# A fused two-block transformer kernel: the first attention's scores as two stacked products of high and low parts

## The chip, the cores and the metric

The kernel runs on one core of one Trainium2 chip. The metric is the device time of one execution in microseconds (us), median of the runs, lower is better. TensorE is called PE below, its weight loads PEld, VectorE DVE, ScalarE ACT, GpSimd POOL and SyncE SP, as in the profile.

## The reference, cut to what matters

Two transformer blocks run one after the other on x of 1024 positions by 1024 channels, all in float32. The part that is changed is the attention of the first block: 8 heads of 64 channels, three dilated windows mixed by their softmax denominators.

```python
z = h @ w_in
q, k, v, zu, zv = jnp.split(z, [D_ATTN, 2 * D_ATTN, 3 * D_ATTN, 3 * D_ATTN + D_SGU], axis=-1)
q = q.reshape(B, S, N_ATTN_HEADS, HEAD_DIM) * (HEAD_DIM ** -0.5)
...
DILATED_BRANCHES = ((128, 1), (512, 4), (2048, 16))
s = jnp.einsum('brnqhd,brnkhd->brnhqk', qb, kw).astype(jnp.float32)
s = s + bias.transpose(2, 0, 1)
...
p = jnp.exp(s - m)
...
w = jax.nn.softmax(jnp.stack(lses, axis=0), axis=0)
return jnp.einsum('ibsh,ibshd->bshd', w.astype(q.dtype), jnp.stack(outs, axis=0))
...
mix = jnp.concatenate([attn, sgu], axis=-1) @ w_out
x = x + rms_norm(mix, g_post_mix)
```

The projection behind that attention (`@ w_out`) is the weight stream that the kernel calls OUT1.

## The kernel before, in words

Everything stands in one program with its waits written by hand; each engine goes through its own list in order. Large products are split: a weight slab `raw` is turned by ACT into a high part `whi` (L768) and by DVE into a low part `wlo` (L1715), both of the reduced-precision type fp32r, and PE adds three fp32r products per tile (L1219, and L1237 where two slabs are interleaved). Slabs alternate between two buffers of each.

The first attention runs over 8 heads with 8 steps each, n = 8h + d. Its pieces, by step:

- **Scores** (L1413): per step two plain float32 products of 128x256, keys `KA` as the weights, queries `QA` as the moving data. For d below 4 (called near here) the 128 keys of a weight load lie side by side; for d of 4 and more (far) they lie 4 elements apart (`far_keys`). Both tiles hold the head's 64 channels in partitions 0 to 63, a row of ones and the guard's row in partition 64 and zeros above.
- **Bias and exponent**: DVE subtracts the bias strip from the scores (L1899), ACT takes the exponent (L913) into one of four `PT` buffers.
- **Weighted values** (L1433 near, L1438 far): three steps behind the scores, float32, summed over a head's steps in TP.
- **Guard** (L1386 on PE, L1885 on DVE): twelve steps ahead, PE forms rounded scores of one 128-row tile and DVE takes a bound from them. After 8 tiles PE (L1393) and ACT (L881, the tile `ROW`) make a row of bounds, and POOL copies it into `QA` by four DMAs (L628). All guard tiles after the first ten share one PSUM tile, so a guard product waits until DVE took the one before. Guards end 12 steps before the last score.

At each head's start ACT has extra work that stands in its list between the exponents: at d = 1 `operands(h+1)` copies keys and queries of the next head (L872, L873), at n = 10, 26 `round_pair` (L861, L862), at d = 2 `sums_copy(h-1)` takes the sums of the head before out of TP (L890), at d = 3 `inverse(h-1)` (L896, L899). PE may not start the weighted values of d = 0 before the first half of that `sums_copy` is done. POOL scales a finished head (L606), moves values (L614) and loads bias and strips.

Around the attention: ACT makes the high part of OUT1's first slab before it, of the second at n = 40; DVE makes their low parts before it and at n = 58.

Of the kernel before, what the change touches and what calls it, by code (L numbers as in the profile page):

```python
# [142 lines left out]
def build(nc, slabs, ada, xT, vecs, lnrow, sgu_wT, rel_bias, positions, consts, hot, outT, dbg=None):  # L143
# [60 lines left out]
    KA = [at(f"KA{b}", [P, S], A_XT + 4096 * b) for b in range(2)]  # L204
    QA = [at(f"QA{b}", [P, S], A_XH + 8192 + 4096 * b) for b in range(2)]
# [120 lines left out]
    zeros_set = sem("zeros_set")  # L326
# [234 lines left out]
    def _(pool):  # L561
# [29 lines left out]
        pool.wait_ge(turned, 16)  # L591
        for b in range(2):
            pool.memset(KA[b][DH:P, :], 0.0).then_inc(zeros_set, 1)
            pool.memset(QA[b][DH:P, :], 0.0).then_inc(zeros_set, 1)
        pool.wait_ge(zeros_set, 4)
        for b in range(2):
            pool.memset(KA[b][DH:DH + 1, :], 1.0).then_inc(ones_set, 1)

# [18 lines left out]
        pool.wait_ge(ones_set, 2)  # L617
# [5 lines left out]
        for h in range(HEADS):  # L623
            pool.wait_ge(row_made, h + 1)
            if h >= 2:
                pool.wait_ge(st_ready, NT * (h - 1))
            for c in range(4):
                pool.dma_start(QA[h % 2][DH:DH + 1, c * 2 * P:(c + 1) * 2 * P],  # L628
                               ROW8[h % 2][0:NT, c * 32:(c + 1) * 32]).then_inc(row_loaded[h % 2], 16)
# [127 lines left out]
    def _(act):  # L757
# [88 lines left out]
        for j in range(4):  # L846

            g = IN1 + S_V1 + j
            hi_next(g, g % 2, g // 2)
# [15 lines left out]
        def operands(h):  # L865
# [26 lines left out]
        def inverse(h):  # L892
# [5 lines left out]
            aseq.wait(act)  # L898
            act.activation(ATTN[h // 2][own, :], OL[h % 2][other, :], ACT.Exp, scale=-1.0).then_inc(inverse_ready, 1)  # L899

        def dilated_attention():

            act.preload_act_table_set("natural_log_exp_and_others")
            operands(0)
# [3 lines left out]
            for n in range(NT * HEADS):  # L908
# [7 lines left out]
                if n == 40:  # L916
                    hi_next(OUT1, OUT1 % 2, OUT1 // 2)
# [6 lines left out]
                if n in (52, 60):  # L924
                    attended(n // 8 - 6)
            sums_copy(HEADS - 1)
# [15 lines left out]
        round_pair(0)  # L942
        turned_hi(4, 4, 16)
# [260 lines left out]
    def _(pe):  # L1204
# [18 lines left out]
        def product_pair(g, xh, xl, fresh, base, order=range(KT_N)):  # L1223

            pe.wait_ge(lo_ready, g + 2)
            for one in (g, g + 1):
                pe.wait_ge(psum_free[one % 2], one // 2 + 1)
            for step in range(KT_N + PAIR_LAG):
                if step < KT_N:
                    pe.wait_ge(fresh, base + step + 1)  # L1230
                for one, at_k in ((g, step), (g + 1, step - PAIR_LAG)):
                    if not 0 <= at_k < KT_N:
                        continue
                    b, k = one % 2, order[at_k]
# [1178 lines left out]
```

## Time and profile before

| | |
|---|---|
| median of 3 runs | 2792.73 us (2788.41 to 2807.02) |
| profiled execution, its own time | 2793.15 us |
| its span | 2791.4 us |
| busy: PE, DVE, ACT, POOL | 2641.2, 1351.2, 836.0, 251.5 us |
| attention, first score to last | 320 to 501 us of the span |

Busy shares are averages; which engine is waited for is read in the stretch itself. A matmul's duration includes its latency, so products that follow each other overlap, and the distance between starts is what one costs. A plain float32 product is two records in the trace, an fp32r one is one record; both carry their own weight load. The profile prints f32 for either.

### The profile page before, as it was taken

To read this page: it belongs to the slowest core of one execution; us is meant where nothing else is said; L and a number is where in the kernel's file an instruction comes from. 1 tells how busy PE (TensorE), PEld (TensorE's weight loads), DVE (VectorE), ACT (ScalarE), POOL (GpSimd) and SP (SyncE) were. 2 spreads that over 40 slices of the span, in tenths; PEclk is the share of its full clock that TensorE was granted. 3 is DMA by queue.
4 is the path that set the end of the run, shared out by engine and by line. 5 is a ranking of instruction groups with operands and counts; after the bars stand their busy time and mean duration, and the time that the engine had idled before them with its cause. 6 is when DMAs were issued, how large, how long until landed. Compare 5 with 4: busy or idle time off the path is not lost.

```text
span 2791.4 us, 28672 instructions
## 1 busy us (share of the span) xinstructions
PE 2641.2 (95%) x11363; PEld 2088.6 (75%) x11363; DVE 1351.2 (48%) x1585; ACT 836.0 (30%) x1083; POOL 251.5 (9%) x269
## 2 busy tenths in 40 slices
PE   5999999989999999999999988898999999999996
PEld 3887667867888888888765766665878888888884
DVE  5242666356334343345748878786453232232333
ACT  3211345333112021121325575435332021120221
POOL 0000222002111121121001000211000000000000
PEclk9999999999999999999899998999999999999997
DMA  3211110214222222231310111001111111111111
GB/s 111 89 46 50 42 55 32 68 60 151 91 80 87 76 90 83 76 105 61 136 41 5 46 39 39 4 8 50 67 38 53 46 46 53 45 53 45 46 53 68
DMA packets 50376, 169.68 MB, mean 61 GB/s; under 512 B 7544, under 2 KB 11128, under 8 KB 50232
## 3 DMA queue, kind: packets, MB, share of 16 engines
q1 hardware_dynamic: 32544, 104.27, 11.4%
q0 software_dynamic: 17728, 63.98, 6.7%
q8 instruction: 72, 1.18, 0.2%
q14 instruction: 32, 0.25, 0.0%
HBM read 152.05 MB, written 12.68 MB: 59 GB/s over the span
## 4 chain that ended last, share of the span: by engine, by line
PE 81%; DVE 9%; ACT 5%; issue 4%; DMA 0%; SPq 0%; DVEq 0%; POOL 0%; ACTq 0%; POOLq 0%
PE G L1219 61%; PE G L1237 4%; PE G L1413 2%; PE TP L1642 2%; ACT TK L1071 2%; PE G L1560 1%; PE TP L1433 1%; PE TP L1386 1%; PE TP L1257 1%; DVE JUNK L2245 1%; PE G L1576 1%; ACT T L1057 1%; PE TP L1280 1%; PE TP L1438 1%; DVE wlo L1715 1%
## 5 line engine op out<-in xcount | busy, mean ns | idle before, releaser
L1219 PE MATMUL G<-XH,whi 128*128 128x512 f32 x1712 | 539.2, 396 | 15.2 <-DVE wlo L1715 13.1
L1219 PE MATMUL G<-XL,whi 128*128 128x512 f32 x1712 | 529.9, 391 | 0.0
L1219 PE MATMUL G<-XH,wlo 128*128 128x512 f32 x1712 | 529.8, 391 | 0.0
L768 ACT ACTIVATE whi<-raw 128x1024 fp32r<-128x1024 f32 x184 | 193.8, 1053 | 732.6 <-PE G L1219 671.0
L1219 PEld LDWEIGHTS G<-XH,whi 128*128 128x128 f32 x1712 | 319.8, 189 | 86.5 <-DVE wlo L1715 15.2
L1219 PEld LDWEIGHTS G<-XL,whi 128*128 128x128 f32 x1712 | 322.7, 189 | 67.8
L1219 PEld LDWEIGHTS G<-XH,wlo 128*128 128x128 f32 x1712 | 322.7, 188 | 67.8
L1219 PE MATMUL G<-UH,whi 128*128 128x512 f32 x1024 | 316.9, 391 | 0.0
L1219 PE MATMUL G<-UL,whi 128*128 128x512 f32 x1024 | 315.6, 389 | 0.0
L1219 PE MATMUL G<-UH,wlo 128*128 128x512 f32 x1024 | 315.5, 389 | 0.0
L1715 DVE TENSOR_TENSOR wlo<-raw,whi 128x1024 fp32r<-128x1024 f32 x184 | 224.3, 1220 | 149.4 <-ACT whi L768 149.1
L1219 PEld LDWEIGHTS G<-UH,wlo 128*128 128x128 f32 x1024 | 192.3, 188 | 40.0
L1219 PEld LDWEIGHTS G<-UL,whi 128*128 128x128 f32 x1024 | 192.3, 188 | 40.0
L1219 PEld LDWEIGHTS G<-UH,whi 128*128 128x128 f32 x1024 | 191.1, 188 | 38.6
L2026 DVE SCALAR_TENSOR_TENSOR XT<-G,mod,XT 128x1024 f32<-128x1024 f32 x32 | 41.1, 1285 | 249.1 <-PE G L1219 249.1
L2012 DVE TENSOR_TENSOR USQ<-RELU 128x1024 f32<-128x1024 f32 x32 | 39.2, 1225 | 192.2 <-ACT RELU L999 192.1
L995 ACT ACTIVATE RELU<-RELU 128x1024 f32<-128x1024 f32 x32 | 34.0, 1062 | 243.1 <-DVE RELU L2006 224.0
L1071 ACT ACTIVATE TK<-SC,cand 128x512 f32<-128x512 f32 (+2 forms) x93 | 82.8, 892 | 67.2 <-DVE cand L2132 67.2
L2026 DVE SCALAR_TENSOR_TENSOR XT<-G,XT 128x1024 f32<-128x1024 f32 x24 | 29.4, 1225 | 151.3 <-PE G L1219 151.3
L1991 DVE TENSOR_REDUCE RED<-ADA 128x128 f32<-128x1024 f32 x48 | 95.0, 1979 | 0.0
L999 ACT ACTIVATE RELU<-G 128x1024 f32<-128x1024 f32 x32 | 32.9, 1028 | 205.0 <-PE G L1219 205.0
L1885 DVE CUSTOM_DVE_ANT_0 JUNK<-TP,BIAS 128x1024 bf16<-128x1024 f32 x54 | 66.2, 1226 | 50.5 <-PE TP L1386 50.5
(304 smaller groups left out, 3195.2 us busy)
## 6 DMA issues: line engine op xcount, KB each, us to landing
raw<-slabs SPq DMA_DIRECT2D x184, 512.0 KB, 3.4
ADA<-ada POOLq DMA_DIRECT2D x48, 512.0 KB, 3.8
x_spill<-XT POOLq DMA_DIRECT2D x2, 4096.0 KB, 12.9
BIAS<-tab_spill POOLq DMA_DIRECT2D x8, 960.0 KB, 4.9
XT<-xT SPq DMA_DIRECT2D x8, 512.0 KB, 10.0
XRE<-xT POOLq DMA_DIRECT2D x8, 512.0 KB, 3.9
XRE<-x_spill POOLq DMA_DIRECT2D x8, 512.0 KB, 3.7
XT<-x_spill POOLq DMA_DIRECT2D x1, 4096.0 KB, 13.8
```

Source lines behind the costliest of these rows:

```text
L768: act.activation(whi[b][:, :, :].rearrange("p k n -> p (k n)"), raw[b][:, :], ACT.Copy).then_inc(hi_ready, 1)
L995: act.activation(RELU[:, :], RELU[:, :], ACT.Square).then_inc(usq_ready, 1)
L1071: t_counted.inc(act.activation((TK1, TK2)[t_counted.n % 2][:, 0:w], SC[:, score_at(TOPK_TILE + n):score_at(TOPK_TILE + n + 1)], ACT.Sign, ...
L1219: last = pe.matmul(G[b][:, half, :], w[b][:, k, :], x[:, k, half * HALF:(half + 1) * HALF], start=(at_k == 0 and n == 0), stop=(at_k == KT ...
L1237: last = pe.matmul(G[b][:, half, :], w[b][:, k, :], x[:, k, half * HALF:(half + 1) * HALF], start=(at_k == 0 and n == 0), stop=(at_k == KT ...
L1413: last = pe.matmul(G[n % 4 // 2][:, n % 2, j * 2 * P:(j + 1) * 2 * P], keys, queries, start=True, stop=True)
L1642: pe.matmul(TP[1][:, u % 2, :], VO2[r][:, c, :], PT2[n % 4][:, :], start=(c == 0), stop=(c == i)).then_inc(p2_used, 1)
L1715: dve.tensor_tensor(wlo[b][:, :, :].rearrange("p k n -> p (k n)"), raw[b][:, :], whi[b][:, :, :].bitcast(F32).rearrange("p k n -> p (k n)" ...
L1885: dve.tensor_tensor_reduce(out=JUNK1[:, :], in0=flat(guard_out(p)), in1=BIAS[h % 2][:, 896 - i * P:896 - i * P + S], scale=1.0, scalar=HIG ...
L1991: dve.tensor_reduce(RED[a % 2][:, :], ADA[a % 2][:, :, :].rearrange("p k n -> p n k"), AX.X, ALU.add).then_inc(ada_red, 1)
L2012: dve.tensor_tensor(USQ[:, :], RELU[:, :], RELU[:, :], ALU.mult).then_inc(usq_ready, 1)
L2026: ins = dve.scalar_tensor_tensor(out=XT[:, m - 8, :], in0=Gf[b], scalar=scale(m - 8), in1=XT[:, m - 8, :], op0=ALU.mult, op1=ALU.add)
```

## The change

Scores are no longer a plain float32 product. Keys and queries are split into an fp32r high part and a low part, and two fp32r products of 128 partitions are added: `KH` (high keys, the same in both halves of the partitions) with `QHL` (high queries in the head's own half, low queries in the other), and `KLO` (low keys in the own half, the row of ones in the other) with `QHR` (high queries in the own half, the guard's row in the other). `KLO` and `QHR` lie where `wlo` and `whi` are, so OUT1's slabs are split at the attention's end.

```diff
-            pool.memset(KA[b][DH:P, :], 0.0).then_inc(zeros_set, 1)
-            pool.memset(QA[b][DH:P, :], 0.0).then_inc(zeros_set, 1)
+            other = halves(b)[1]
+            one = ones[other, :].unsqueeze(1).broadcast_to([DH, NT, P])
+            for t in (KLO, QHR):
+                pool.tensor_tensor(t[b][other, :].rearrange("p (t c) -> p t c", c=P), one, one, ALU.subtract).then_inc(zeros_set, 1)
...
+        def low_parts(h):
+
+            own, other = halves(h)
+            pool.wait_ge(ones_set, 4 if h else 2)
+            if h:
+                pool.wait_ge(values_ready, max(h, 2))
+            if h > 2:
+                pool.wait_ge(att_scaled, h - 2)
+            pool.wait_ge(operands_ready, 4 * (h + 1))
+            pool.tensor_tensor(KLO[h % 2][own, ::-1], KT[own, h // 2, :], KH[h % 2][own, ::-1].bitcast(F32),
+                               ALU.subtract).then_inc(lows_ready, 1)
+            in_class = lambda t: t.rearrange("p (c u) -> p c u", c=4)
+            pool.wait_ge(lows_ready, 2 * h + 1)
+            pool.tensor_tensor(in_class(QHL[h % 2][other, :]), by_class(QT[own, h // 2, :]),
+                               in_class(QHL[h % 2][own, :].bitcast(F32)), ALU.subtract).then_inc(lows_ready, 1)
...
         for h in range(HEADS):
+            if h:
+                low_parts(h)
             pool.wait_ge(row_made, h + 1)
...
-                act.wait_ge(operands_ready, 4)
+                act.wait_ge(operands_ready, 8)
+                act.wait_ge(lows_ready, 4)
...
-            act.activation(KA[h % 2][0:DH, ::-1], KT[own, h // 2, :], ACT.Copy).then_inc(operands_ready, 1)
-            act.activation(QA[h % 2][0:DH, :].rearrange("p (c u) -> p c u", c=4), by_class(QT[own, h // 2, :]),
-                           ACT.Copy).then_inc(operands_ready, 1)
+            for at_p in halves(h):
+                act.activation(KH[h % 2][at_p, ::-1], KT[own, h // 2, :], ACT.Copy).then_inc(operands_ready, 1)
+            for q in (QHL, QHR):
+                act.activation(q[h % 2][own, :].rearrange("p (c u) -> p c u", c=4), by_class(QT[own, h // 2, :]),
+                               ACT.Copy).then_inc(operands_ready, 1)
...
+            if h < 2:
+                act.wait_ge(lows_ready, 2 * (h + 3))
             act.activation(ATTN[h // 2][own, :], OL[h % 2][other, :], ACT.Exp, scale=-1.0).then_inc(inverse_ready, 1)
...
-                if n == 40:
-                    hi_next(OUT1, OUT1 % 2, OUT1 // 2)
+                if n == NT * (HEADS - 1) + 1:
+                    act.wait_ge(st_ready, NT * (HEADS - 1))
+                    hi(OUT1, OUT1 % 2, OUT1 // 2)
...
+            act.wait_ge(st_ready, NT * HEADS)
+            hi(OUT1 + 1, (OUT1 + 1) % 2, (OUT1 + 1) // 2)
             sums_copy(HEADS - 1)
...
         round_pair(0)
+        operands(0)
         turned_hi(4, 4, 16)
...
             for j in range(2):
...
-                last = pe.matmul(G[n % 4 // 2][:, n % 2, j * 2 * P:(j + 1) * 2 * P], keys, queries, start=True, stop=True)
+                for n_part, (k, q) in enumerate(((KH, QHL), (KLO, QHR))):
...
+                    last = pe.matmul(G[n % 4 // 2][:, n % 2, j * 2 * P:(j + 1) * 2 * P], keys, queries,
+                                     start=(n_part == 0), stop=(n_part == 1))
...
-                if n == NT * HEADS - 6:
-                    lo(OUT1 + 1, (OUT1 + 1) % 2)
+                if n == NT * HEADS - 5:
+                    lo(OUT1, OUT1 % 2)
+            lo(OUT1 + 1, (OUT1 + 1) % 2)
```

At a head's start ACT's list reads as follows, before: the exponent of n = 9, the operands of head 2, the exponent of n = 10, the pair that `round_pair` makes, and the copy of head 0's sums.

```order
L913 ACTIVATE PT_100<-PT_100 128x512
L872 ACTIVATE KA_91<-KT 64x1024
L873 ACTIVATE QA_93<-QT 64x1024
L913 ACTIVATE PT_101<-PT_101 128x512
L861 ACTIVATE KR_97<-KT 128x1024
L862 ACTIVATE QR_95<-QT 128x8x128
L890 ACTIVATE OL_103<-TP 128x512 x2
```

The same place after the change.

```order
L945 ACTIVATE PT_104<-PT_104 128x512
L902 ACTIVATE KH_91<-KT 64x1024 x2
L904 ACTIVATE QHL_93<-QT 64x1024
L904 ACTIVATE QHR_97<-QT 64x1024
L945 ACTIVATE PT_105<-PT_105 128x512
L890 ACTIVATE KR_101<-KT 128x1024
L891 ACTIVATE QR_99<-QT 128x8x128
L921 ACTIVATE OL_107<-TP 128x512 x2
```

Two copies became four, ahead of the copy of the sums (`OL<-TP`). On PE a near step, before: two products of scores, the weighted values, the guard.

```order
L1413 MATMUL G<-QA_93,KA_91 128x256 x2
L1438 MATMUL TP<-PT_100,VONE_106 128x128 x4
L1386 MATMUL TP<-KR_98,QR_96 128x512 x2
L1413 MATMUL G<-QA_93,KA_91 128x256 x2
L1438 MATMUL TP<-PT_101,VONE_106 128x128 x4
L1386 MATMUL TP<-KR_98,QR_96 128x512 x2
```

The same step after.

```order
L1453 MATMUL G<-QHL_93,KH_91 128x256
L1453 MATMUL G<-QHR_97,KLO_95 128x256
L1453 MATMUL G<-QHL_93,KH_91 128x256
L1453 MATMUL G<-QHR_97,KLO_95 128x256
L1479 MATMUL TP<-PT_105,VONE_110 128x128 x4
L1424 MATMUL TP<-KR_102,QR_100 128x512 x2
```

Four products with alternating weights stand where two stood. On POOL the list ahead of the first row of bounds, before:

```order
L593 MEMSET KA_91 64x1024
L594 MEMSET QA_93 64x1024
L593 MEMSET KA_92 64x1024
L594 MEMSET QA_94 64x1024
L597 MEMSET KA_91 1x1024
L597 MEMSET KA_92 1x1024
L614 COPY VONE_105<-VV 128x16x64
L622 MEMSET VONE_105 128x16x64
L614 COPY VONE_106<-VV 128x16x64
L622 MEMSET VONE_106 128x16x64
L628 DMA QA_93<-ROW_0_89 1x8x32 x4
```

And after:

```order
L599 TENSOR_TENSOR KLO_95<-cst 64x1024
L599 TENSOR_TENSOR QHR_97<-cst 64x1024
L599 TENSOR_TENSOR KLO_96<-cst 64x1024
L599 TENSOR_TENSOR QHR_98<-cst 64x1024
L604 TENSOR_TENSOR KLO_95<-cst 1x1024
L604 TENSOR_TENSOR KLO_96<-cst 1x1024
L615 TENSOR_TENSOR KLO_95<-KT,KH_91 64x1024
L619 TENSOR_TENSOR QHL_93<-QT,QHL_93 64x1024
L638 COPY VONE_109<-VV 128x16x64
L646 MEMSET VONE_109 128x16x64
L655 DMA QHR_97<-ROW_0_89 1x8x32 x4
```

Six memsets became six two-input operations, and two subtractions were put in ahead of the values and the row.

## Rows read from the trace of the kernel before

**Rows 1.** The attention stretch as one window: busy time of each engine, granted clock.

```profile
320.00:501.00 181.00, 170.28 (x760) 126.63 (x759) 118.04 (x170) 86.19 (x117) 44.25 (x52) 0.96 0.13 44
```

**Rows 2.** Timeline of PE: start, us, line, tiles, records, idle before and its releaser.

```profile
386.54 1.31 PE L1413 MATMUL G<-QA,KA 128*128 128x256 f32 x4
387.69 1.03 PE L1433 MATMUL TP<-PT,VONE 128*128 128x256 f32 x4
...
392.09 1.13 PE L1413 MATMUL G<-QA,KA 128*128 128x256 f32 x4
...
394.70 1.13 PE L1413 MATMUL G<-QA,KA 128*128 128x256 f32 x4
...
403.64 2.05 PE L1433 MATMUL TP<-PT,VONE 128*128 128x256 f32 x4 [2.58 <-ACT OL L890]
...
406.76 2.10 PE L1413 MATMUL G<-QA,KA 128*128 128x256 f32 x4
408.79 0.60 PE L1393 MATMUL TP<-cst,nega 128*8 128x128 f32 x2
...
427.60 1.13 PE L1413 MATMUL G<-QA,KA 128*128 128x256 f32 x4
429.65 1.10 PE L1433 MATMUL TP<-PT,VONE 128*128 128x256 f32 x4 [0.92 <-ACT OL L890]
...
452.92 1.10 PE L1433 MATMUL TP<-PT,VONE 128*128 128x256 f32 x4 [0.68 <-ACT OL L890]
```

**Rows 3.** Timeline of ACT at two starts of a head.

```profile
424.74 0.63 ACT L913 ACTIVATE PT<-PT 128x512 f32<-128x512 f32 x1 [1.97 <-DVE PT L1899]
425.39 1.05 ACT L872 ACTIVATE KA<-KT 64x1024 f32<-64x1024 f32 x1
426.35 2.02 ACT L873 ACTIVATE QA<-QT 64x1024 f32<-64x1024 f32 x1
428.39 0.63 ACT L913 ACTIVATE PT<-PT 128x512 f32<-128x512 f32 x1
...
448.23 0.63 ACT L913 ACTIVATE PT<-PT 128x512 f32<-128x512 f32 x1 [1.04 <-DVE PT L1899]
```

**Rows 4.** Timeline of PE in the last head's approach, where no guards are left.

```profile
484.72 1.09 PE L1413 MATMUL G<-QA,KA 128*128 128x256 f32 x4
485.65 1.05 PE L1438 MATMUL TP<-PT,VONE 128*128 128x128 f32 x8
486.54 1.03 PE L1413 MATMUL G<-QA,KA 128*128 128x256 f32 x4
487.40 1.05 PE L1438 MATMUL TP<-PT,VONE 128*128 128x128 f32 x8
```

**Rows 5.** Weight loads by line and shape, windows 385:391 (far) and 392:400 (near).

```profile
L1413 PEld LDWEIGHTS G<-QA,KA 128*128 128x128 f32 x8 | 2.0, 325 | 0.7 <-issue 0.7
L1413 PEld LDWEIGHTS G<-QA,KA 128*128 128x128 f32 x13 | 2.2, 189 | 1.6 <-DVE PT L1899 1.1 <-issue 0.4
```

**Rows 6.** Merged chain of waits: 32 float32 records of 128 columns, 96 fp32r of 512.

```profile
501.25 3.57 PE TP L1438 x32
504.82 21.80 PE G L1237 x96
```

**Rows 7.** Groups of POOL by line and shape, whole span.

```profile
L670 POOL TENSOR_TENSOR ADA<-ADA,silc 128x1024 f32<-128x1024 f32 x44 | 84.0, 1910 | 14.7 <-DMA ADA<-ada 13.8
L606 POOL TENSOR_TENSOR QT<-OL,QT 64x1024 f32<-64x1024 f32 x6 | 14.2, 2362 | 20.4 <-ACT QT L899 19.8
```

**Rows 8.** Timeline ahead of the attention and at its first steps.

```profile
292.95 0.94 POOL L593 MEMSET KA<- 64x1024 f32 x1 [38.56 <-PE TP L1350]
...
297.75 1.02 ACT L939 ACTIVATE XH<-TP 128x1024 fp32r<-128x1024 f32 x1 [6.48 <-PE TP L1367]
...
312.90 2.04 POOL L628 DMA_DIRECT2D QA<-ROW  x4 [4.80 <-ACT ROW L881]
...
327.38 1.03 PE L1433 MATMUL TP<-PT,VONE 128*128 128x256 f32 x4
```

More of the change, by code:

```diff
@@ L203, in build @@
     ROW8 = [at(f"ROW8_{b}", [P, P], A_XT + 29696 + 512 * b) for b in range(2)]
-    KA = [at(f"KA{b}", [P, S], A_XT + 4096 * b) for b in range(2)]
-    QA = [at(f"QA{b}", [P, S], A_XH + 8192 + 4096 * b) for b in range(2)]
+    KH = [at(f"KH{b}", [P, S], A_XT + 4096 * b, F32R) for b in range(2)]
+    QHL = [at(f"QHL{b}", [P, S], A_XH + 8192 + 4096 * b, F32R) for b in range(2)]
+    KLO = [at(f"KLO{b}", [P, S], A_WLO + 4096 * b, F32R) for b in range(2)]
+    QHR = [at(f"QHR{b}", [P, S], A_WHI + 4096 * b, F32R) for b in range(2)]
     QR = [at("QR0", [P, S], A_XH, F32R), at("QR1", [P, S], A_R, F32R)]
@@ L591, in _ @@
         pool.wait_ge(turned, 16)
+        pool.wait_ge(slab_done, 1 + OUT1)
         for b in range(2):
-            pool.memset(KA[b][DH:P, :], 0.0).then_inc(zeros_set, 1)
-            pool.memset(QA[b][DH:P, :], 0.0).then_inc(zeros_set, 1)
+            other = halves(b)[1]
+            one = ones[other, :].unsqueeze(1).broadcast_to([DH, NT, P])
+            for t in (KLO, QHR):
+                pool.tensor_tensor(t[b][other, :].rearrange("p (t c) -> p t c", c=P), one, one, ALU.subtract).then_inc(zeros_set, 1)
         pool.wait_ge(zeros_set, 4)
         for b in range(2):
-            pool.memset(KA[b][DH:DH + 1, :], 1.0).then_inc(ones_set, 1)
+            row = halves(b)[1].start
+            one = ones[row:row + 1, :].unsqueeze(1).broadcast_to([1, NT, P])
+            pool.tensor_tensor(KLO[b][row:row + 1, :].rearrange("p (t c) -> p t c", c=P), one, one, ALU.mult).then_inc(ones_set, 1)
+        def low_parts(h):
[12 more added lines that the diff above has]
+                               in_class(QHL[h % 2][own, :].bitcast(F32)), ALU.subtract).then_inc(lows_ready, 1)
+            pool.wait_ge(lows_ready, 2 * h + 2)
         def scale_head(h):
@@ L626, in _ @@
                 pool.wait_ge(st_ready, NT * (h - 1))
+            row = halves(h)[1].start
             for c in range(4):
-                pool.dma_start(QA[h % 2][DH:DH + 1, c * 2 * P:(c + 1) * 2 * P],
+                pool.dma_start(QHR[h % 2][row:row + 1, c * 2 * P:(c + 1) * 2 * P],
                                ROW8[h % 2][0:NT, c * 32:(c + 1) * 32]).then_inc(row_loaded[h % 2], 16)
@@ L1234, in product_pair @@
                     b, k = one % 2, order[at_k]
+                    if (one, at_k) == (g + 1, 0):
+                        pe.wait_ge(lo_ready, g + 2)
                     for n, (w, x) in enumerate(((whi, xh), (whi, xl), (wlo, xh))):
@@ L1398, in scores_by_key @@
             if d == 0:
-                pe.wait_ge(operands_ready, 2 * (h + 1))
+                pe.wait_ge(operands_ready, 4 * (h + 1))
+                pe.wait_ge(lows_ready, 2 * (h + 1))
                 pe.wait_ge(row_loaded[h % 2], 64 * (h // 2 + 1))
```

24 lines of the change are left out of this document (12 added, 12 removed).

## The prediction

> **What bounds the kernel now.** The change touches only the first attention and its two edges, so I read that stretch as one window first [rows 1]: in 181 us PE is busy for 170, DVE for 118, ACT for 86, POOL for 44, and the granted clock is 0.96 of full. Then I followed PE's timeline [rows 2] for a wait. Inside a head there is none: the reader should see starts without a bracket, a near step coming every 2.61 us (392.09 to 394.70). At every head's start there is one: the weighted values of d = 0 wait for ACT's copy of the sums, 2.58 us at 403.64 (a head with `round_pair` in it), 0.92 at 429.65, 0.68 at 452.92. So PE sets the pace inside a head, and ACT's list sets when the next one may go on. The change cuts PE's work and adds to ACT's list at just that place.
>
> ACT's way to that point [rows 3]: exponent of d = 1 at 424.74, key copy 425.39, query copy 426.35, exponent of d = 2 at 428.39, then the sums, and PE goes on at 429.65 [rows 2]. From that exponent to PE it is 4.91 us, of which the operands are 0.96 + 2.04 = 3.00.
>
> **What a score product costs.** Before, a step has two products, four records. Without guards between, a near step's scores take 487.40 - 486.54 = 0.86, a far step's 485.65 - 484.72 = 0.93 [rows 4], 0.215 and 0.233 for a record. Both move the same 256 columns, so the array's work is equal and the far one is held by something else. The weight loads say by what: 325 ns each where keys lie 4 elements apart, 189 ns where they are side by side [rows 5]. Such a load can be repeated much more often than it is long: 32 float32 records of 128 columns take 3.57 us, 0.112 each [rows 6]. If the far load's extra 325 - 189 = 136 ns is occupation of the load path, a far load can be repeated every 0.112 + 0.136 = 0.248, and 0.233 is what far records show. I take it that far scores are bound by weight loads.
>
> After, a step has four fp32r products, again four records with four loads. The column work halves. Near: between 0.112 (the loads' pace) and half of an fp32r record of 512 columns plus its excess, 21.80 / 96 = 0.227, so some 0.12 [rows 6]. Saving 4 x (0.215 - 0.12) = 0.38 us per near step. Far: the loads are as many and as strided, so 0.233 stays and the saving is 0; its other end is also 0.38, if the far load is only late and not occupying. I take 0, since 0.233 lies beside 0.248 and not beside 0.215.
>
> [...]
>
> **The change part by part.**
>
> *Near steps.* Where does a shorter one move an end? The sequence up to the exponent of d = 1 runs over the guard that PE issues at the end of step d = 0, so of the near scores only d = 0 moves that exponent; those of d = 1, 2, 3 run into the wait for the sums. With n = 3 of the first head (the only other near step with weighted values and no such wait behind it) that is 7 x 0.38 = 2.7 us saved. In the last head there are no guards and no operands, so its four count: 1.5 us. Together -4.2.
>
> *Four copies for two on ACT.* Each time `operands(h+1)` is made at d = 1 (h = 1 to 6), ACT has another key copy (0.96) and another query copy (2.04, or 1.97 by the second head start) ahead of the sums. PE already waits there, so all of it is on the path: 2.95 x 6 = +17.7 us. This is the main term. It is hidden by nothing: the wait for the copy of the sums is the last to end at every one of these places.
>
> *The clock behind a longer wait.* [...] What a fall costs: from the weighted values of d = 0 to the next head's exponent of d = 1 it is 424.74 - 403.64 = 21.10 with a fall, 448.23 - 429.65 = 18.58 without [rows 2, 3], so 2.5. Falls stand now at two of the six (heads 1 and 3, those with `round_pair`). After, PE waits 0.9 + 2.95 + what the near steps gave (two or three times 0.38), so 4.4 to 5 us, at all of the other four, and longer than 2.58 at each. A fall would cost less than 2.5 then: the far scores in it take 408.79 - 406.76 = 2.03 against 387.69 - 386.54 = 1.15 [rows 2], since at half the clock columns bind again; with half the columns that comes off, 0.8. So four new falls at 1.7 = +6.8, and the two old ones cheaper by 0.8 each = -1.6. Ends for a fall: 1.7 and 2.5, and 0 if none came.
>
> *Start of the attention.* On ACT `operands(0)` moves ahead of the copies at 297.75, into an idle of 6.48 us that begins at 291.27 [rows 8]. It can start once the transposes of values are over, at 292.95 (where POOL starts), and takes 2 x 0.96 + 2 x 2.0 = 5.9, to 298.9: those copies come 1.1 us later. On POOL, six memsets of 0.94 become two-input operations of 1.91 to 2.36 us [rows 7], and two subtractions and 4 us of values follow: 292.95 + 8 x (1.91 to 2.36) + 4.0 = 312.2 to 315.9, where the row's DMAs started at 312.90 [rows 8] and would start at 314.0 by ACT's shift. First scores were at 320, the four DMAs take 2 us, so there is cover of 3 us and I charge 1.0 us for the whole start. POOL then subtracts for head 1 as soon as ACT has its operands (312.90 + 1.1 + 5.9 = 320) and is done by 325; ACT's `round_pair(1)`, and behind it the exponent of n = 0, wait for that, to 327. PE asks for that exponent at its fourth step, 327.38 before [rows 8] and 328 after: just covered.
>
> *Waits of ACT for POOL in the first two inverses* (`lows_ready` at h < 2). POOL needs 2 x 2.36 = 4.7 us after the operands; ACT gets there after 3.0 (after 4.9 with `round_pair`). It stalls 1.7 us once, behind the sums, ahead of exponents that PE wants three steps later. 0. The row of later heads: POOL is free 4.7 us after the operands, the row is made after d = 4, later than that. 0.
>
> *Splits of OUT1.* One high part (1.04 on ACT) now stands at d = 1 of the last head ahead of its sums: +0.3, since exponents there are not dense. The other high part and both low parts fall beside the last weighted values (3.57 us) and the first tiles of the interleaved product, which needs the second slab only two tiles in. 0.
>
> Sum: 17.7 + 6.8 - 1.6 - 4.2 + 1.0 + 0.3 = **+20.0 us**, on the profiled execution's own 2793.15: 2813.2. The median is 0.4 lower than that execution, so I forecast **2813 us**.
>
> **The rivals.**
>
> *Far steps gain too* (the second case). 28 far steps with guards at PE's pace and 4 in the last head, 32 x 0.38 = 12.2 less: +8, 2801 us. For it: the latency of a load needn't be its occupation. Against it: near and far records differ in pace and only their loads differ [rows 4, 5].
>
> *No more falls of the clock*: +20 - 6.8 = +13, 2806 us. For it: nothing but that waits between 2.6 and 5 us do not occur in this stretch. Against: 2.58 is enough already.
>
> *Not slower, on the other side: scores nearly vanish from PE's path.* Its place is the step inside a head. With guards between, a far step's scores stand for 1.15 us, of which 0.93 is work and the rest a load that nothing covers. If strided loads of fp32r keys ran side by side and those of the second product were hidden under the first, a step could fall to some 0.4, a saving of up to 0.75 far and 0.5 near. The costs without any gain in the steps are 20.0 + 4.2 = 24.2; over the 28 + 4 far and 11 near steps that count (43) it turns at 0.56 a step. At 0.7 it is 24.2 - 30.1 = -6, 2787 us. Against it: four loads remain, and 0.45 is the least that near loads show.
>
> *POOL's small operations are dear.* Strided or partition-moving two-input operations could cost twice the 2.36: then eight of them at the start end at 292.95 + 37.8 + 4 = 334.7 instead of 315.9, first scores come 17 us later, and the time is 2830 us. At a head's start the slack is 8 us and holds. For it: ACT's query copy shows that such a pattern can double a time (2.04 against 0.96) [rows 3]. Against: four of the eight are broadcasts, like the row of 1.91.
>
> **How the numbers follow.** Chances: forecast 0.47 (2806 to 2822, by the ends of the falls, of the start and of the near steps), far gain 0.17, no falls 0.08, not slower 0.13, POOL dear 0.15. The range from 2796 to 2829 leaves out the case below and half of the dearest. One per cent is 28 us, about what a measurement here can tell from no change: slower by more means above 2820.7, which takes POOL dear and the upper edge of the forecast, 0.24; faster by more, below 2764.8, would need more than PE's scores cost in 60 steps, 0.03; within, 0.73.
>
> **What would show it.** In the profile after: the wait for the copy of the sums at heads 1 to 6 at 4 to 6 us, with doubled records behind each; near scores at 0.5 per step and far at 0.93 in the last head; weight loads of far keys at 325 ns still; two copies of 0.96 and two of 2.0 in ACT's list; the attention longer by 20 us, and nothing else changed. The prediction is wrong if far scores fall to 0.5 as well, if the waits come out short, or if first scores come later than 322.

## The result, and the profile after

The changed kernel takes 2836.6 us (median of 4 runs, 2834.52 to 2848.56) against 2792.7 us: 1.0163 times as long, 95% interval 1.014 to 1.0187. That is +44 us where +20 was forecast, and outside the range. The profiled execution took 2848.56 us, some 12 us more than the kernel's other three runs; its profile is read with that in mind.

Three windows of the changed kernel tell where the time lies: from the first score to the first product of OUT1, the 31 us ahead of it, and a stretch of 2276 us behind it (columns as in rows 1).

```profile
331.80:561.63 229.83, 192.57 (x792) 141.74 (x790) 118.94 (x170) 106.93 (x133) 75.87 (x64) 0.73 0.11 35
...
301.00:332.00 31.00, 31.00 (x76) 19.16 (x75) 13.95 (x21) 11.17 (x10) 19.52 (x15) 0.50 0.10 32
...
570.00:2846.00 2276.00, 2173.05 (x9301) 1729.36 (x9299) 1105.24 (x1267) 659.97 (x860) 186.54 (x187) 0.98 0.19 61
```

The same three windows of the kernel before.

```profile
320.24:504.57 184.33, 173.61 (x791) 129.99 (x790) 118.50 (x171) 86.82 (x118) 44.25 (x52) 0.96 0.13 43
...
301.00:320.00 19.00, 18.43 (x64) 10.85 (x65) 12.91 (x20) 11.60 (x10) 6.41 (x9) 0.82 0.15 52
...
515.00:2791.00 2276.00, 2170.99 (x9292) 1728.74 (x9290) 1105.33 (x1266) 659.92 (x860) 185.25 (x185) 0.98 0.19 61
```

Behind the attention next to nothing changed: from the first product of OUT1 to the end it is 2285.3 us, and 2286.8 before, and in windows of equal length PE is busy for 2173 and 2171 us. The attention is 45.5 us longer, and its granted clock went from 0.96 to 0.73. Read in windows of 1 us from 300 to 600, it is 1.00 in 137 of them and 0.50 in 149, and between the two only in the 14 where it changes. With these two levels, full and half, a mean of 0.73 means that 2 x 0.27 = 54% of 229.8 us ran at half the clock, 124 us against some 15 before. The first score comes 11.6 us later; the clock stood at 0.50 through all of the window ahead of it.

The waits, of PE in that stretch (us in total, times, longest); before it was 9.3 in 7, the longest 2.6.

```profile
PE TP L1474 <- ACT OL L921: 35.3, 7, 6.8
```

PE's timeline of the changed kernel, from the start of one head to the start of the next, answers to rows 2.

```profile
369.32 2.05 PE L1474 MATMUL TP<-PT,VONE 128*128 128x256 f32 x4 [6.81 <-ACT OL L921]
371.30 1.22 PE L1424 MATMUL TP<-KR,QR 64*128 64x512 f32 x2
...
377.62 0.60 PE L1453 MATMUL G<-QHL,KH 128*128 128x256 f32 x1
...
378.73 2.12 PE L1474 MATMUL TP<-PT,VONE 128*128 128x64 f32 x6
...
381.93 0.60 PE L1453 MATMUL G<-QHL,KH 128*128 128x256 f32 x1
...
392.98 1.15 PE L1424 MATMUL TP<-KR,QR 64*128 64x512 f32 x2
...
394.63 1.05 PE L1479 MATMUL TP<-PT,VONE 128*128 128x128 f32 x8
...
404.43 2.04 PE L1474 MATMUL TP<-PT,VONE 128*128 128x256 f32 x4 [5.19 <-ACT OL L921]
```

What to see: behind the wait no row has a bracket, PE goes from one instruction to the next, and still the weighted values take 2 us instead of 1 and the guard 1.22 instead of 0.73, until 393. A far step takes 381.93 - 377.62 = 4.31 us. At the full clock it takes 2.78 (shown below), so each costs 1.5 us more, for 24 us on end. Before, the records behind the wait at 403.64 were back to their usual length within 7 us.

ACT's timeline at the next head starts (answers to rows 3).

```profile
396.41 0.63 ACT L945 ACTIVATE PT<-PT 128x512 f32<-128x512 f32 x1 [3.25 <-DVE PT L1940]
...
429.55 0.63 ACT L945 ACTIVATE PT<-PT 128x512 f32<-128x512 f32 x1 [1.60 <-DVE PT L1940]
430.09 2.12 ACT L902 ACTIVATE KH<-KT 64x1024 fp32r<-64x1024 f32 x2
432.24 2.02 ACT L904 ACTIVATE QHL<-QT 64x1024 fp32r<-64x1024 f32 x1
434.17 1.99 ACT L904 ACTIVATE QHR<-QT 64x1024 fp32r<-64x1024 f32 x1
...
438.48 1.05 ACT L921 ACTIVATE OL<-TP 128x512 f32<-128x512 f32 x2
...
493.09 0.63 ACT L945 ACTIVATE PT<-PT 128x512 f32<-128x512 f32 x1 [1.58 <-DVE PT L1940]
```

```profile
439.20 2.05 PE L1474 MATMUL TP<-PT,VONE 128*128 128x256 f32 x4 [6.82 <-ACT OL L921]
...
500.85 2.04 PE L1474 MATMUL TP<-PT,VONE 128*128 128x256 f32 x4 [4.92 <-ACT OL L921]
```

Here the forecast held. From the exponent of d = 1 to PE it is 500.85 - 493.09 = 7.76 us. At the same head it was 452.92 - 448.23 = 4.69 before [rows 2, 3], so two more copies cost 3.07 where 2.95 was forecast. With a rounded pair it is 439.20 - 429.55 = 9.65, and 6.58 before. The six heads give 3.07 to 3.11 each.

### The profile page after: what moved, and what is told of

Read it like the earlier page. It is cut to its first block, busy times and chain, and to the rows that moved or that the text cites. A ratio compares the mean times of both kernels' runs of the same rounds, so it can differ in the third digit from the quotient of the medians.

```text
span 2846.9 us, 28721 instructions
## 1 busy us (share of the span) xinstructions
PE 2672.9 (94%) x11363; PEld 2107.2 (74%) x11363; DVE 1350.8 (47%) x1585; ACT 859.7 (30%) x1099; POOL 299.3 (11%) x285
## 4 chain that ended last, share of the span: by engine, by line
PE 80%; DVE 9%; ACT 6%; issue 4%; DMA 0%; SPq 0%; DVEq 0%; POOL 0%; ACTq 0%; POOLq 0%
PE G L1255 60%; PE G L1275 4%; PE TP L1474 2%; PE TP L1683 2%; ACT TK L1107 2%; PE TP L1424 1%; PE G L1453 1%; PE G L1601 1%; DVE JUNK L2287 1%; PE G L1617 1%; PE TP L1295 1%; PE TP L1479 1%; ACT T L1093 1%; PE TP L1318 1%; PE TP L1290 1%
```

## The experiments

Twelve kernels were run, three rounds each. The ratio is to the kernel before as it was timed beside each of them (its medians went from 2790.8 to 2795.6 us), so it is the ratios that compare across rows. Their starts differ from run to run in ways the change has no part in (below), so beside the median the table gives the profiled execution's attention, first score to first product of OUT1: its length, the granted clock in that window, what of it was at half the clock (twice what the clock lacks, times the length), and PE's waits in it for the copy of the sums, with waits that took their place behind a plus.

| kernel | median us | ratio to before, 95% | attention us | clock | at half clock, us | waits us |
|---|---|---|---|---|---|---|
| before | 2792.7 | 1 | 184.3 | 0.96 | 15 | 9.3 |
| after | 2836.6 | 1.014 to 1.019 | 229.8 | 0.73 | 124 | 35.3 |
| e1_fill | 2824.4 | 1.010 to 1.014 | 202.3 | 0.93 | 28 | 8.1 |
| e2_copies | 2829.2 | 1.011 to 1.017 | 218.1 | 0.85 | 65 | 27.1 |
| e3_less | 2816.6 | 1.007 to 1.014 | 210.8 | 0.75 | 105 | 16.7 |
| e4_order | 2831.5 | 1.013 to 1.016 | 217.7 | 0.84 | 70 | 5.0 + 36.5 |
| e6_spread | 2827.2 | 1.007 to 1.013 | 223.2 | 0.73 | 121 | 5.2 + 16.3 |
| e7_before_spread | 2788.2 | 0.996 to 1.000 | 177.9 | 0.97 | 11 | 4.2 |
| e8_cols | 2840.9 | 1.012 to 1.022 | 223.5 | 0.82 | 80 | 35.3 |
| e9_split | 2791.5 | 0.997 to 1.002 | 183.4 | 0.97 | 11 | 9.3 |
| e10_clear | 2783.2 | 0.992 to 0.998 | 166.5 | 0.97 | 10 | 5.1 + 1.8 |
| e11_clear_cols | 2789.7 | 0.995 to 0.998 | 179.2 | 0.92 | 29 | 5.1 + 0.5 |
| e12_before_clear | 2773.6 | 0.989 to 0.995 | 169.9 | 1.00 | 0 | 0.7 |
| e13_side | 2766.7 | 0.984 to 0.994 | 157.2 | 0.97 | 9 | 5.1 + 2.9 |

**e1_fill: work in the place of the wait.**

```diff
+        def keep_busy(n, count):
+            pe.wait_ge(st_taken, n - 2)
+            for _ in range(count):
+                pe.matmul(G[(n + 1) % 4 // 2][:, (n + 1) % 2, :], XH[:, 4, 0:P], XH[:, 4, 0:HALF], start=True, stop=True)
...
+                if n % NT == PV_BEHIND and n // NT in (1, 2, 3, 4, 5, 6):
+                    keep_busy(n, 20)
```

> The changed kernel, with 20 idle fp32r products of 512 columns put into PE's list at d = 3 of heads 1 to 6, just ahead of the weighted values that wait for the copy of the sums. They write a score tile that is overwritten later. Theory A (the excess over the forecast is the lower clock that follows each long wait of PE): the products fill the wait at 0.23 us each (4.6 of some 5 to 6 us), the clock stays up behind it, the weighted values of d = 0 take 1.1 us instead of 2.05, the low stretches of 10 to 27 us behind them go, and the time falls from 2836 to between 2800 and 2815 us, although work was added. Theory B (the excess is in ACT's and POOL's work itself, the clock only follows): the time stays within 5 us of the changed kernel's 2836 or rises.

It added 120 products and came out 12 us faster than the changed kernel; its profiled attention is 229.8 - 202.3 = 27.5 us shorter. Where the fill covers the wait, the weighted values behind it take 1.10 again:

```profile
393.74 1.10 PE L1480 MATMUL TP<-PT,VONE 128*128 128x256 f32 x4 [0.66 <-ACT OL L921]
```

ACT's list is the same, and so is its way to the copy of the sums; what changed is PE's clock behind it, 1.00 from 394 to 418 us where the changed kernel has 0.50 from 405 to 423. So a good part of the loss is the low clock and not the wait. The median is 9 us above the range that was expected. Two heads with rounded pairs still wait 2.3 us, with a low clock behind it (0.50 in the window 366 to 374); what else is in it isn't shown (the executions without a profile took some 8 us more than the profiled one).

**e2_copies: the copies alone, scores as before.**

```diff
+            if h > 1:
+                act.activation(KA[h % 2][0:DH, ::-1], KT[own, h // 2, :], ACT.Copy).then_inc(twice, 1)
+                act.activation(QA[h % 2][0:DH, :].rearrange("p (c u) -> p c u", c=4), by_class(QT[own, h // 2, :]),
+                               ACT.Copy).then_inc(twice, 1)
+                act.wait_ge(twice, 2 * (h - 1))
```

> The kernel before (plain float32 scores), with the operand copies of heads 2 to 7 made twice on ACT, one set after the other: the same added ACT work at the same place as in the change (some 3.1 us each), and nothing else of it. Theory A1 (the clock stays low for long because PE's wait is long): waits of 4 to 6 us, low stretches as long as in the changed kernel, 2793 plus 18 for the copies plus 20 or more, 2830 to 2840 us. Theory A2 (the clock stays low for long because fp32r scores give PE half the columns per step, so that it comes back late): waits as long, but low stretches of some 7 us as the kernel before has behind its wait of 2.6 us, and 2793 + 18 + 4 x 2.5 = 2821 us, between 2815 and 2826.

**e3_less: the products alone.** The changed kernel with two of the four copies for heads 2 to 7 left out, so the operands' other halves there are an earlier head's and its scores are not the reference's.

```diff
-            for at_p in halves(h):
+            for at_p in halves(h)[:2 if h < 2 else 1]:
...
-            for q in (QHL, QHR):
+            for q in (QHL, QHR)[:2 if h < 2 else 1]:
```

> The changed kernel without two of the four operand copies of heads 2 to 7: the keys are copied into one half of KH only and the queries into QHL only, so the second product of those heads works on old data, and its output differs from the reference. All else, the subtractions on POOL and the four products, stays. Theory A1: waits of PE are back at 0.7 to 1 us (2.6 with the rounded pair), clock falls at two heads at most, and the lighter scores show their gain: 2793 - 4 = 2789, between 2783 and 2796 us. Theory A2: light scores keep the clock low wherever it falls, so two or three low stretches are still 10 us or longer: 2795 to 2808 us.

The copies alone cost 38 us on the kernel before, the products alone 26. Against what was expected, e2_copies lies between its two cases, and e3_less above both of its own. The two don't add up to the change's 44, and both have the low clock in them. What each does to the clock is read from the weighted values behind one wait and the 25 us that follow it; first e2_copies (float32 scores), then e3_less (fp32r).

```profile
389.42 2.05 PE L1438 MATMUL TP<-PT,VONE 128*128 128x256 f32 x4 [3.90 <-ACT OL L895]
...
389.00:414.00 25.00, 24.59 (x98) 17.70 (x98) 14.25 (x21) 9.26 (x14) 6.74 (x8) 0.83 0.17 56
```

```profile
384.05 2.05 PE L1474 MATMUL TP<-PT,VONE 128*128 128x256 f32 x4 [2.10 <-ACT OL L921]
...
384.00:409.00 25.00, 24.86 (x94) 17.54 (x95) 12.97 (x19) 7.23 (x12) 11.29 (x10) 0.67 0.16 56
```

The longer wait, with float32 scores behind it, leaves 2 x 0.17 x 25 = 8.5 us at half the clock; the shorter one, with fp32r scores, 16.5. PE is as busy in both. A wait in e3_less nearly as long as the one of e2_copies leaves 24:

```profile
352.39 1.61 PE L1474 MATMUL TP<-PT,VONE 128*128 128x256 f32 x4 [3.71 <-ACT OL L921]
...
352.00:377.00 25.00, 24.52 (x72) 16.97 (x73) 10.00 (x16) 6.77 (x11) 9.57 (x9) 0.52 0.15 56
```

Over the attention it is 65 us with waits of 27 and 105 us with waits of 17. So it is not the waits' length that makes the low clock last; it goes with the light scores. The two kernels also differ in POOL's list, where only e3_less has the subtractions.

**e4_order: the copies behind the sums.**

```diff
-                if n in (10, 26):
+                if n in (12, 28):
...
-                if d == 1 and 1 <= h < HEADS - 1:
-                    operands(h + 1)
                 if d == 2 and h:
                     sums_copy(h - 1)
+                if d == 2 and 1 <= h < HEADS - 1:
+                    operands(h + 1)
```

> The changed kernel with ACT's list in another order: the four operand copies of the next head stand behind the copy of the sums at d = 2 instead of ahead of it at d = 1, and the rounded pair at n = 12 and 28 instead of 10 and 26. No work is added or taken away. Theory A (the four copies cost only since they stand ahead of the sums, and the falls only follow the waits): PE's waits at the heads' starts go, no clock falls at them, 6 x 7.9 us of ACT's way and the near steps' gain come off: 2836 - 45 - 15, between 2765 and 2790 us, under the kernel before. Theory B (ACT's or POOL's added work binds wherever it stands): over 2810 us.

A clear miss. The waits for the sums are 0.65 us each, and others stand in their place. ACT, then PE:

```profile
397.88 1.05 ACT L932 ACTIVATE KT<-OL 64x1024 f32<-64x1024 f32 x1 [4.30 <-POOL QHL L619]
398.96 0.27 ACT L912 ACTIVATE ROW<-TP 8x128 f32<-8x128 f32 x1
```

```profile
399.32 1.19 PE L1424 MATMUL TP<-KR,QR 64*128 64x512 f32 x2 [9.23 <-issue]
```

The next guard on PE needs the row's place in PSUM free, and the row stands in ACT's list behind the copies and the inverse. In heads 1 and 2 the inverse also waits for POOL's subtraction, which waits for the copies: 8.6 and 9.2 us. In heads 3 to 5 the copies alone are enough for 4.7 to 5.0 us each. The last wait, 4.3 us, is that of head 7's first score for its row's DMAs, which stand behind POOL's subtractions. It is 36.5 us in all, and the clock falls behind them as before (0.84 in the mean over the attention, 70 us at half of it).

**e6_spread, e7_before_spread: the copies one at a time,** on the changed kernel and (keys at d = 4, queries at d = 5) on the one before; POOL's subtractions wait for the parts they read.

```diff
-                if d == 1 and 1 <= h < HEADS - 1:
-                    operands(h + 1)
+                if 4 <= d < 7 and 1 <= h < HEADS - 1:
+                    operands(h + 1, (d - 4,))
...
-                if d == 3 and h:
+                if d == 3 and h > 2:
                     inverse(h - 1)
+                if d == 0 and h in (2, 3):
+                    inverse(h - 2)
```

> The kernel after, with the four copies of the next head's operands spread over three later steps (two key copies behind d = 4, one query copy behind d = 5, one behind d = 6) instead of all behind d = 1, and the first two inverses moved to d = 0 of heads 2 and 3, so that they don't stand in ACT's list while POOL still subtracts. Nothing else stands between the exponents of d = 1 and 2 except the two pairs of rounded tiles. My theory (the added wait for the copy of the sums, and the low clock that it starts, are the whole loss): waits of 0.6 to 0.7 us at heads 1 to 6 except 3 to 4 at heads 1 and 3, the granted clock full at the others, and the time near 2770 us (2760 to 2790): 6 times 3 us of wait and 5 of low clock less than the last variant's 2824 to 2831. Rival (the light score products alone let the clock fall, whatever the waits): waits as short, the granted clock still 0.5 to 0.7 behind heads' starts, and 2795 to 2820.

> The kernel before, with its two operand copies moved in the same way (keys behind d = 4, queries behind d = 5) and the first two inverses at d = 0 of heads 2 and 3; scores stay plain float32. The wait for the sums goes from 0.7 to 2.6 us down to 0.6 or less, the first head's by some 3 us: 2775 to 2790 us, and the granted clock 1.00 through the attention. Beside the fp32r kernel with the same order it tells what the score products give by themselves: by the near steps alone some 4 us plus 8 for the starts of heads, by the rival of light products a loss.

e6_spread missed as well, and again a queue was behind it. POOL, then PE:

```profile
410.49 2.90 POOL L620 TENSOR_TENSOR QHL<-QT,QHL 64x1024 fp32r<-64x1024 f32 x1 [1.19 <-ACT QHL L905]
413.69 2.02 POOL L656 DMA_DIRECT2D QHR<-ROW  x4 [0.30 <-POOL QHL L620]
```

```profile
416.93 0.55 PE L1456 MATMUL G<-QHL,KH 128*128 128x256 f32 x1 [3.23 <-issue]
...
430.42 2.04 PE L1477 MATMUL TP<-PT,VONE 128*128 128x256 f32 x4 [0.28 <-ACT OL L922]
```

The row of bounds had been ready since 404; its four DMAs stood behind the subtractions in POOL's list, and the next head's first score waited for them. The second row of PE tells more: its own wait is 0.28 us, but the weighted values take 2.04, since the clock had not come back since the wait 13 us earlier (it is 0.50 from 417 to 446). There are four such waits of 3.1 to 5.8 us, 16.3 us with two small ones. They don't account for all of the 121 us at half the clock: some 27 of them lie in head 0, ahead of the first of these waits (more on this under e10_clear). My theory was that the waits for the copy of the sums, with the clock behind them, were "the whole loss"; cut to 5.2 us they left the kernel 33 us slower than before. e7_before_spread, where POOL's list has no subtractions, shows no such wait, and with float32 scores the clock is 0.97.

**e8_cols: more work in the far steps.**

```diff
+            for _ in range(2 if d >= 4 and 1 <= h <= 6 else 0):
+                pe.matmul(G[n % 4 // 2][:, n % 2, :], XH[:, 4, 0:P], XH[:, 4, 0:HALF], start=True, stop=True)
```

> The kernel after, with two idle fp32r products of 512 columns ahead of each far step's scores in heads 1 to 6 (they write the tile that the scores then overwrite, and change no result). They are 2 x 0.22 = 0.44 us of work in each of 24 far steps, 10.6 us at the full clock if none of it is covered. Theory A (the chip keeps the low clock because the far steps hold too little column work, even though PE has no idle time in them): stretches at the low clock behind each head's start shrink from 14 to 27 us to under 10, which gives back more than the added work, 2815 to 2830. Rival (the length of the wait alone sets how long the low clock lasts): stretches as long as they were, and 2845 to 2860.

Between the two. Waits are the same 35.3 us, 10.6 us of work came on top, and the time at half the clock fell from 124 to 80 us, though single heads still had 20; the median rose by 4 us, with an interval of 14 to either side, so it decides little by itself. It agrees in direction with the light scores holding the clock down. The extra products don't bring the time at half the clock down to the 65 us of e2_copies.

**e9_split: the other half of the change,** the splits of OUT1 moved as in the changed kernel, scores as before.

> The kernel before, with only the other half of the change: the splits of OUT1's two slabs moved to the end of the attention, product and waits as in the changed kernel. By the forecast's terms +0.3 us, so 2788 to 2796. If this half costs more (the second slab's parts late for the interleaved product), PE waits at that product's start and the stretch from the last head's first weighted values to it is longer than 11.1 us.

Ratio 0.9995: this half costs nothing, as forecast. Its profile also settles the late start. With POOL's old list ahead of the attention, the window 296 to 320 had the clock at 0.52 in this execution, and the first score came at 325.5:

```profile
296.00:320.00 24.00, 24.00 (x67) 15.44 (x65) 12.47 (x18) 10.21 (x10) 5.98 (x8) 0.52 0.00 1
```

e2_copies, with float32 scores as well, has the same 0.52 there. So a fall there doesn't need the change; the profile of the changed kernel has it too. That kernel's other runs, 12 us shorter at a mean granted clock of 0.957 to 0.960 against 0.952, probably had less of it.

**e10_clear, e11_clear_cols, e12_before_clear: every known wait taken away.** The diff is against e6_spread; e11_clear_cols adds the two products of e8_cols, and e12_before_clear has ACT's part of it on the kernel before.

```diff
-            if h:
+            if h == 1:
                 low_parts(h)
             pool.wait_ge(row_made, h + 1)
...
                                ROW8[h % 2][0:NT, c * 32:(c + 1) * 32]).then_inc(row_loaded[h % 2], 16)
+            if h > 1:
+                low_parts(h)
...
-                if n in (10, 26):
+                if n in (15, 31):
                     round_pair(n // 16 + 2)
-                if 4 <= d < 7 and 1 <= h < HEADS - 1:
-                    operands(h + 1, (d - 4,))
+                if 3 <= d < 6 and 1 <= h < HEADS - 1:
+                    operands(h + 1, (d - 3,))
...
-                if d == 3 and h > 2:
+                if d == 6 and h > 2:
                     inverse(h - 1)
```

> The kernel after, with every known wait at a head's start taken out of the queues: on ACT the next head's operands stand at d = 3, 4, 5, the inverse at d = 6 (the first two at d = 0 of heads 2 and 3), the rounded pairs at n = 15 and 31; on POOL the row's four DMAs stand ahead of the low parts from head 2 on, so that PE no longer waits for them behind a subtraction (3.2 and up to 5.8 us in the variant with spread operands). Theory 1 (the waits are the seed of every stretch at the low clock, the light scores only make it long): waits under 1 us, at most two short low stretches after the first head, 2775 to 2795 us. Theory 2 (light score products alone bring or keep the low clock, waits or not): waits as short, stretches at the low clock of 17 to 37 us remain at several heads, 2810 to 2830.

> The same kernel with two idle fp32r products of 512 columns ahead of each far step's scores in heads 1 to 6 (24 steps, 0.44 us each, 10.6 us in all at the full clock, overwritten by the scores). Theory 1: 10 us slower than the variant without them, no change in the clock, 2785 to 2805. Theory 2: the low stretches go to those of float32 scores, and it is 10 us or more faster than the variant without them, 2795 to 2810.

> The kernel before (plain float32 scores) with ACT's list in the same order: operands at d = 3 and 4, the inverse at d = 6, rounded pairs at n = 15 and 31. Waits for the sums 0.6 us or less at every head and no low clock in heads 1 to 6: 2780 to 2788 us. It is the yardstick for what fp32r scores give when nothing else is in their way: Theory 1 has them 0 to 8 us faster or slower than this, Theory 2 some 30 slower.

This is the deciding run. e10_clear has the fp32r products of the changed kernel, all four copies and both subtractions, and takes 2783 us, 53 less than the changed kernel and 12 less than before. Its far steps, and its window from 370 to 395:

```profile
370.00:395.00 25.00, 24.16 (x125) 17.96 (x125) 19.82 (x31) 17.00 (x21) 13.72 (x11) 1.00 0.18 57
```

```profile
380.03 0.51 PE L1458 MATMUL G<-QHL,KH 128*128 128x256 f32 x1
...
382.81 0.51 PE L1458 MATMUL G<-QHL,KH 128*128 128x256 f32 x1
...
396.23 1.10 PE L1479 MATMUL TP<-PT,VONE 128*128 128x256 f32 x4 [0.67 <-ACT OL L924]
```

For heads 1 to 7 theory 1 holds: with waits of 0.65 us at the starts of heads 1 to 6 (1.8 and 1.2 only at the last) the clock stays full, light scores or not (1.00 from 337 to 560). Theory 2 expected stretches at the low clock at several heads and 2810 us or more, and neither came. e11_clear_cols took 2790, 6 us more than e10_clear and within what theory 1 expected.

Head 0 is another matter. There the clock falls in all nine kernels with fp32r scores, behind waits of PE for a guard's place that are 1.07 us at most, and in none of the five with float32 scores, whose waits there are 0.66 or less. It stays low (0.50) for 10 us in e10_clear and for 27 in e11_clear_cols, whose heads 1 to 6 alone have the extra products. First e11_clear_cols, then the same stretch of e12_before_clear.

```profile
330.26 0.73 PE L1429 MATMUL TP<-KR,QR 64*128 64x512 f32 x2 [0.84 <-DVE nega L1933]
...
332.37 1.22 PE L1429 MATMUL TP<-KR,QR 64*128 64x512 f32 x2 [0.71 <-DVE nega L1933]
...
332.00:358.00 26.00, 25.54 (x74) 17.93 (x74) 13.38 (x21) 4.32 (x8) 3.34 (x6) 0.50 0.16 54
```

```profile
320.00:346.00 26.00, 24.94 (x109) 17.72 (x107) 19.92 (x30) 5.93 (x10) 3.29 (x6) 1.00 0.16 54
```

So with light scores two waits under 1 us can go with a low clock of 27 us. From head 1 on every fall within the attention, in any of the kernels, had a wait of 1.8 us or more ahead of it. Whether in head 0 it is the short waits or the scores themselves isn't shown.

e12_before_clear is the best version that computes the reference: 2773.6 us, 0.992 of the time before, and faster than was expected. Per head at the full clock the fp32r kernel is faster, 21.4 us from 374.84 to 396.23 against 22.4 (395.12 to 417.56), and its profiled attention is 3.4 us shorter. Its median is 10 us longer all the same; the mean granted clock of its executions is 0.968 to 0.976 against 0.973 to 0.981. In which stretch the executions without a profile lose this isn't shown.

**e13_side: far keys side by side.**

```diff
-                        keys, queries = far_keys(k, 2 * c + j), q[:, c * 2 * P:(c + 1) * 2 * P]
+                        keys, queries = k[:, (2 * c + j) * P:(2 * c + j + 1) * P], q[:, c * 2 * P:(c + 1) * 2 * P]
```

> The variant with all waits cleared, with one thing changed: the far steps' weight loads take 128 keys side by side instead of 4 elements apart (so these scores are of other keys, and the output is not the reference's). Columns, loads, operands and waits are the same in number. If the distance of the keys in a load is what holds far steps at 0.233 us per product against 0.117 near, far products now repeat every 0.117 too, loads last 189 instead of 325 ns, and each of 28 far steps in heads 1 to 7 is 0.46 us shorter: head to head 19.5 instead of 21.4 us and 2768 to 2775 us, unless the still lighter steps let the clock fall. If far steps are held by something else (the queries' order, the target bank), nothing changes: 2783.

Weight loads of far steps (window 379 to 388), e10_clear and then e13_side:

```profile
L1458 PEld LDWEIGHTS G<-QHR,KLO 128*128 128x128 f32 x6 | 2.0, 330 | 0.0
```

```profile
L1458 PEld LDWEIGHTS G<-QHR,KLO 128*128 128x128 f32 x8 | 1.5, 188 | 0.0
```

The loads take 188 ns instead of 330, far products start 0.12 us apart instead of 0.23, a head takes 397.45 - 377.49 = 19.96 us instead of 21.4, and the time is 2767 us, under what was expected. Nothing else was changed, so the distance of the keys in a load is the cause.

## Why the prediction was wrong, step by step

**Score products: right.** Near products start 0.12 us apart and far ones 0.23, in the changed kernel itself (far, then near):

```profile
347.31 0.40 PE L1453 MATMUL G<-QHR,KLO 128*128 128x256 f32 x1
347.55 0.40 PE L1453 MATMUL G<-QHL,KH 128*128 128x256 f32 x1
...
355.33 0.28 PE L1453 MATMUL G<-QHR,KLO 128*128 128x256 f32 x1
355.45 0.28 PE L1453 MATMUL G<-QHL,KH 128*128 128x256 f32 x1
```

0.12 and 0.233 were forecast, and e13_side shows the reason to be the one given: with the keys side by side a far load takes 188 ns instead of 330, and far products start 0.12 us apart. The case "far steps gain too" is out, and so is "not slower" by its mechanism.

**Four copies for two: right.** +2.95 us each was forecast and 7.76 - 4.69 = 3.07 measured, 18.5 us for the six heads where 17.7 was forecast. All waits together grew by 35.3 - 9.3 = 26.0 us: the copies' 18.5, and the near steps' savings that ran into the wait, as said.

**Splits and POOL: right.** e9_split gives 0 for the splits. POOL's operations were not dear (2.36 and 2.89 us, where 2.36 was the most assumed), and the row's DMAs waited for ACT and not for them:

```profile
303.55 2.36 POOL L615 TENSOR_TENSOR KLO<-KT,KH 64x1024 fp32r<-64x1024 f32 x1
305.99 2.89 POOL L619 TENSOR_TENSOR QHL<-QT,QHL 64x1024 fp32r<-64x1024 f32 x1
...
319.86 2.08 POOL L655 DMA_DIRECT2D QHR<-ROW  x4 [6.05 <-ACT ROW L912]
```

**The clock behind a longer wait: this step failed.** The forecast took its falls from the one profile before, where the granted clock is 0.50 from 404 to 408, behind the wait of 2.58 us, and 1.00 from 430 to 448 and from 453 to 470, behind those of 0.92 and 0.68. "Four new falls at 1.7" and "the two old ones cheaper by 0.8 each" came to +5.2 us; what was left of the 44 is about 30. From the weighted values of d = 0 to the next exponent of d = 1 the five heads took 27.1, 25.1, 23.7, 22.1 and 23.6 us (such as 396.41 - 369.32), against 17.9 to 18.5 at the full clock (e10_clear, 18.1 in the mean), so a fall cost 4.0 to 9.0, 6.2 in the mean. The count of falls was right for heads 1 to 6, each has one; the fall in head 0, some 10 us at the low clock, was not foreseen. Wrong was to take the price from the one fall in the profile before and scale what lay inside it. I argued that a lighter score is cheaper at half the clock, and that holds: scores of a far step take 378.73 - 377.62 = 1.11 us there, not 2.03. That it is the columns that hold a score there was my estimate. But a fall's price is mostly its length, and that didn't stay: it went from 7 us to 24 behind the wait at 369.32. The longer waits have the smaller part in that: with float32 scores behind waits of 3.7 to 5.6 us (e2_copies) the same five falls cost 2.6 to 5.0 us, 3.5 in the mean, against 18.58 at the full clock. With fp32r scores behind waits of 1.8 to 3.7 us (e3_less) they cost 2.2 to 8.6, 6.4 in the mean, as much as in the changed kernel. So the rest came with the lighter scores, near products of 0.12 us where float32 records took 0.215 (and in direction e8_cols).

**The start.** 1.0 us was charged, 11.6 is in the profile, from a fall of the clock that e9_split also has with the old start. How much of it is in the median's +44 isn't shown. Where the clock was at 1.00 from 240 to 317 us, the first score came at 317.78 with the new start (e3_less) and at 317.07 with the old one (e7_before_spread). That is 0.7 us, so the charge of 1.0 was about right.

So for the medians: 18.5 for the copies less the 4.2 forecast for near steps is 14, and some 30 are left, which I put down to the clock. The 27.5 us by which the profiled attention of e1_fill is shorter, with the copies all there, agree.

**What stays open:** why the clock, once low, comes back after 7 us with float32 scores (403.64) and after 24 with fp32r ones (369.32) while PE is without a gap in both; e8_cols alone doesn't settle it, and no run had fp32r scores without POOL's subtractions. What lets the clock fall in head 0, for 3 to 27 us, with fp32r scores only. And the 10 us between e10_clear and e12_before_clear.

## What to carry to other kernels

Ahead of a change that lengthens a wait of PE, count the wait twice: its length, and the stretch at half the clock behind it, whose length went with what PE does there; behind waits of 3.7 and 3.9 us it was 24 us with the lighter products and 8.5 without. When work is added to ACT or POOL, place it piece by piece where that queue has slack, and follow everything queued behind it: here the kernel with four copies in one block was 44 us slower than before, and the one with them spread over three steps and POOL's list in another order was 12 us faster, but two orders in between only moved the wait to another semaphore. Compare such a kernel with the old one in the same order too: lighter products gave 1.0 us per head at the full clock here, and the float32 kernel without waits was still 10 us faster. Where keys are read with a stride, look at the load's pace first: 330 ns a load with keys 4 elements apart here, 188 with keys side by side.

## What the runs showed of the hardware that was not expected

- PE without any gap can stay at half the clock for long: from 369.32 to 393 us in the changed kernel, where no row has a bracket, the window 370 to 392 has a granted clock of 0.50 and PE is busy for 21.91 of its 22 us.
- The low clock at 430.42 in e6_spread had no wait of its own (0.28 us): it was the tail of a fall 13 us earlier. The wait printed beside a doubled record need not be its cause.
- Two extra fp32r products of 512 columns in each far step cost 22.5 - 21.4 = 1.1 us per head of four such steps (heads at 387.44 and 409.94 in e11_clear_cols), where 4 x 0.44 = 1.8 was expected.
- Waits of 0.84 and 0.71 us in head 0 of e11_clear_cols had 27 us at half the clock behind them, while in heads 1 to 6 it stayed full behind waits of 0.65 (1.00 from 360 to 560).
- Far fp32r scores at the full clock are bound by loads to a degree that one address pattern is worth 16 us of the whole kernel (e13_side against e10_clear, medians).
